# TensorE's order in the attention rounds: the projection piece ahead of the next scores

## The chip, the cores and the metric

One core of a Trainium2 chip runs the whole program. The metric is device time in microseconds (us); lower is better. TensorE (PE) multiplies, VectorE (DVE) and ScalarE (ACT) read its results from PSUM, GpSimd (POOL) works between buffers in SBUF, and SyncE (SP) issues loads. Each engine works off its own instructions in the order in which they stand; semaphores are all that ties the engines to each other.

## The reference, cut to what matters

Two transformer-like blocks run one after the other on 1024 tokens of width 1024, in float32. The change is inside the second block's attention: sixteen heads of width 64, eight of them stick-breaking ("s") and eight forgetting attention ("f").

```
h = rmsnorm_2(x, attn_norm_g)
proj = h @ w_in
# "s" heads, strictly causal:
z = q @ k.T * 0.125
log_one_minus = where(mask, log_sigmoid(-z), 0)
after = cumsum(log_one_minus, reverse=True) - log_one_minus
o = where(mask, exp(log_sigmoid(z) + after), 0) @ v
# "f" heads, causal, F = cumsum(log_sigmoid(f_logit + bias)):
o = softmax(q @ k.T * 0.125 + F[t] - F[s]) @ v
```

## The kernel before, in words

Attention is done in eight **rounds** of two heads each; "s" and "f" rounds take turns, an "s" round first. A round has sixteen **tiles**, eight for each of its two heads: tile t of a head is 128 query rows against (t mod 8) + 1 blocks of 128 keys, so the work grows along eight tiles and falls back at the ninth. While TensorE works on the tiles of one round it also makes the projections (q, k, v) of the next: 18 **pieces** a round, P0 to P17 below, of nine or six matmuls of 512 columns (line 2062). Three pieces make one **half** (512 tokens of q, k or v), and all halves share one PSUM bank, the lower half of G0 (J in the code). VectorE takes a finished half out of it ("evac", line 2478, the rows named `projected<-G`), and the first piece of the next half (P0, P3, P6, P9, P12, P15) waits for that.

The order on TensorE is a loop written out by hand, one turn for each **step** n = 0 to 15 of a round. Before the change a step is: the scores of tile n, two tiles ahead of the one whose weights are due (`scores(s + 2)`; lines 2089, 2090 and the mask 2092); the piece of the step (`PIECE_AT`); the values of tile n - 3 (line 2120); the transposes of tile n - 2 (line 2102). Step 1 has the transposes of v between, step 4 those of the finished round's output (line 2141), and steps 6 and 14 have a second piece, P7 and P16, at their end. Scores alternate between the banks S2 and G1; their first matmul waits until the tile two earlier was read out of the same bank, and at step 5 also until ScalarE has copied the output's transposes (`outT`, line 2307), which use the upper half of G1.

For an "s" tile ScalarE makes 1 - sigmoid (`not_taken`, line 2281; the name reads `forget_sums<-G` for every second tile, which is written to that buffer), VectorE scans it (line 2515), ScalarE makes sigmoid (`taken`, line 2286) when the probability buffer is free, and VectorE multiplies (line 2518). For an "f" tile VectorE adds the forget sums (line 2508, `first`) once GpSimd has put the mask into them (lines 1988, 1990), and ScalarE takes the exponential (line 2292). Either result is what the transposes wait for; ScalarE copies the transposes (`p copied`, line 2275), and the values wait for that.

VectorE's own order has the evacuations between the tiles: the first before the work of tile 2 (step 3), then at steps 6, 8, 11, and 13 in rounds of odd number (14 in even ones), and step 0 of the next. The one of step 8 stands behind the low part of q (line 2486), the one of step 13 or 14 behind the low part of k (line 2493). Rounds here are numbered by the projections under way: in odd rounds (1, 3, 5, 7) the tiles are "s" tiles, in even rounds (2, 4, 6) "f" tiles. Round 0 has pieces only and the last round tiles only.

Of the kernel before, what the change touches and what calls it, by code (L numbers as in the profile page):

```python
# [159 lines left out]
def program(nc, a, out, known):  # L160
# [290 lines left out]
    with nc.Block() as block:  # L451
# [925 lines left out]
        def _(v):  # L1377
# [46 lines left out]
            def exponents(h, w):  # L1424
                s = LEVELS[w - 1]
                me(f"stage {w - 1} k", h)
                fv, fl, fr = block_view(F, s)
                bv, bl, br = block_view(B, s)
                fb, bb = broadcast(fv[:, :, s - 1:s], s), broadcast(bv[:, :, s:s + 1], s)
                _, kl, kr = block_view(E[0], s)  # L1430
                _, ql, qr = block_view(E[1], s)
                v.tensor_tensor(kl, fb, fl, ALU.subtract)
                S.mark("dve", f"exponents {w} 0", v.tensor_tensor(kr, br, bb, ALU.subtract), h)  # L1433
                me(f"stage {w - 1}", h)
                v.tensor_tensor(ql, bb, bl, ALU.subtract)
                S.mark("dve", f"exponents {w} 1", v.tensor_tensor(qr, fr, fb, ALU.subtract), h)
# [192 lines left out]
        @block.gpsimd  # L1629
        def _(g):  # L1630
            split_pair(J_BRB, 0)
            for name, j0, _, _ in BRANCHES:
                splits_of(j0, first=1 if name == "brb" else 0)
# [90 lines left out]
        TILES, STEPS, SHIFT = 2 * TT, 2 * TT * 2 * HEADS, 2  # L1724
# [41 lines left out]
        def tile_of(g):  # L1766

            return X[g // TILES % 2], g % TILES // TT, g % TT
# [11 lines left out]
        def mask_in_sums(g):  # L1780

            return tile_of(g)[0] == "f" and g // TILES < ROUNDS - 1
# [7 lines left out]
        def stream(s):  # L1790

            q, n = divmod(s + SHIFT, TILES)
            return q + 1, n
# [223 lines left out]
        def _(pe):  # L2017
# [25 lines left out]
            def rstd_spread(name, dst, src):  # L2043
                S.wait(pe, "dve", f"{name} diagonals")
                S.mark("pe", f"{name} spread", over_features(halves_of(dst), src))

            def piece(q, p):

                h, part = divmod(p, 3)
                j, half = J_ATT + 3 * q + h // 2, h % 2  # L2050
                bank = FIRST_BANKS[h] if q == 0 else J
                if part == 0:
                    if half == 0:
                        pe.wait_ge(w_ready, j + 1)
                    if q == 0 and h == 2:
                        S.wait(pe, "dve", "f projected")
                    elif q or h > 3:
                        S.wait(pe, "dve", "evac", 6 * q + h - (2 if q == 0 else 1))
                cols = slice(half * NB, half * NB + NB)
                for k in (range(0, 3), range(3, 6), range(6, 8))[part]:  # L2060
                    for w, m, first, last in ((w_hi, A[0], k == 0, False), (w_hi, A[1], False, False), (w_lo, A[0], False, k == KT - 1)):
                        mm = pe.matmul(bank, w[:, j % 2, k, :], m[:, k, cols], start=first, stop=last)  # L2062
                if part == 2 and half == 0:
                    S.mark("pe", "half", mm, 6 * q + h)
                elif part == 2:
                    mm.then_inc(gemm_done, 1)

            def read(g):

                S.wait(pe, *(("dve", "first", g) if tile_of(g)[0] == "f" else ("act", "taken", g)))  # L2070

            def scores(g):

                x, hh, tt = tile_of(g)
                r = g // TILES
                (Qh, Ql, Ks, _), z, w = SETS[r % 2], Z[g % 2], (tt + 1) * P
                if g < 2:
                    S.wait(pe, "act", ("rstd12 copied", "rstd1 copied")[g], 1)
                else:
                    read(g - 2)  # L2080
                if g > TILES and g % TILES == 5:
                    S.wait(pe, "act", "outT", 2 * (r - 1))
                if g % TILES == 0:
                    S.wait(pe, "act", "k high", r)
                    S.wait(pe, "dve", "k low", r)
                t = slice(tt * P, (tt + 1) * P)
                for b in range((w + NB - 1) // NB):
                    cols = slice(b * NB, min(w, (b + 1) * NB))
                    pe.matmul(z[:, cols], Qh[hh][:, t], Ks[hh][:, cols], start=True, stop=False)  # L2089
                    mm = pe.matmul(z[:, cols], Ql[hh][:, t], Ks[hh][:, cols], start=False, stop=mask_in_sums(g) or tt // 4 != b)  # L2090
                if not mask_in_sums(g):
                    mm = pe.matmul(z[:, tt * P:w], identb, maskb[:, "fs".index(x), :], start=False, stop=True)
                S.mark("pe", "z", mm, g)

            def turned(g):

                S.wait(pe, "act" if tile_of(g)[0] == "f" else "dve", "made", g)
                for c, b0, n in GROUP_AT[g]:
                    S.wait(pe, *U_FREE[U_AT["p", c] - 2])
                    bank = bank_of_u(("p", c))  # L2100
                    for b in range(n):
                        mm = pe.transpose(bank[:, b * P:(b + 1) * P], pr[g % 2][:, (b0 + b) * P:(b0 + b + 1) * P], ident)  # L2102
                    S.mark("pe", "turned", mm, c)

            def values(g):


                _, hh, tt = tile_of(g)
                r, at = g // TILES, g % 4 * HD
                v = SETS[r % 2][3]  # L2110
                if g == 0:
                    S.wait(pe, "dve", "evac", 5)
                elif g % 4 == 0:
                    S.wait(pe, "dve", "out", g // 4 - 1)
                if g % TILES == 0:
                    S.wait(pe, "act", "v copied", 2 * r + 1)
                for c, b0, n in GROUP_AT[g]:
                    S.wait(pe, "act", "p copied", c)
                    for b in range(n):
                        mm = pe.matmul(V[:, at:at + HD], pT[c % 2][:, b, :], v[:, b0 + b, own_rows(hh)], start=b0 + b == 0, stop=b0 + b == tt)  # L2120
                    S.mark("pe", "values", mm, c)

            def v_turned(r):
                for half in range(2):
                    S.wait(pe, "dve", "evac", 6 * r + 4 + half)
                    u = U_AT["v", 2 * r + half]
                    if u >= 2:
                        S.wait(pe, *U_FREE[u - 2])
                    for b in range(4):
                        mm = pe.transpose(U[u % 2][:, b * P:(b + 1) * P], qt[:, (4 * half + b) * P:(4 * half + b + 1) * P], ident)  # L2130
                    S.mark("pe", "v turned", mm, 2 * r + half)

            def out_turned(r):
                S.wait(pe, "dve", "out", 4 * r + 3)
                for half in range(2):
                    if ("o", 2 * r + half) in U_AT:
                        S.wait(pe, *U_FREE[U_AT["o", 2 * r + half] - 2])
                    else:
                        read(TILES * (r + 1) - 1)
                    for b in range(4):  # L2140
                        mm = pe.transpose(bank_of_out(r, half)[:, b * P:(b + 1) * P], ON[:, 4 * half + b, :], ident)
                    S.mark("pe", "out turned", mm, 2 * r + half)

            for s in range(-TILES - SHIFT, STEPS):
                q, n = stream(s)
                if 0 <= s + 2 < STEPS:
                    scores(s + 2)
                if q == 0 and n == 0:
                    rstd_spread("rstd12", S2, bs[:, 0, :])
                if q == 0 and n == 3:  # L2150
                    rstd_spread("rstd1", G[1], bs[:, 1, :])
                if q < ROUNDS:
                    piece(q, PIECE_AT[n][0])
                if n == 1 and 1 <= q <= ROUNDS:
                    v_turned(q - 1)
                if s >= 1:
                    values(s - 1)
                if s > TILES and s % TILES == 2:
                    out_turned(s // TILES - 1)
                if s >= 0:  # L2160
                    turned(s)
                if q < ROUNDS:
                    for p in PIECE_AT[n][1:]:
                        piece(q, p)
# [1235 lines left out]
```

## Time and profile before

| | |
|---|---|
| median of 3 runs | 2547.94 us (2546.5 to 2552.3) |
| profiled execution, its own time | 2548.83 us |
| span of its trace | 2547.0 us |
| TensorE matmul busy | 2499.9 us, 98% of the span |
| VectorE, ScalarE, GpSimd busy | 60%, 40%, 42% |
| share of TensorE in the chain that ended last | 83% |
| that chain at the pieces, line 2062 | 10% |
| at the values, line 2120 | 5% |
| granted TensorE clock, mean | 0.996 |

The attention rounds with both pieces and tiles run from about 1233 to 1712 us of the span. A round takes some 68 to 70 us. TensorE's busy time counts a matmul from its start to a modelled end, so matmuls that follow each other overlap in it; how long work holds the engine is better read from one start to the next.

### The profile page before, as it was taken

To read this page: it belongs to the slowest core of one execution; us is meant where nothing else is said; L and a number is where in the kernel's file an instruction comes from. 1 tells how busy PE (TensorE), PEld (TensorE's weight loads), DVE (VectorE), ACT (ScalarE), POOL (GpSimd) and SP (SyncE) were. 2 spreads that over 40 slices of the span, in tenths; PEclk is the share of its full clock that TensorE was granted. 3 is DMA by queue.
4 is the path that set the end of the run, shared out by engine and by line. 5 is a ranking of instruction groups with operands and counts; after the bars stand their busy time and mean duration, and the time that the engine had idled before them with its cause. 6 is when DMAs were issued, how large, how long until landed. Compare 5 with 4: busy or idle time off the path is not lost.

```text
span 2547.0 us, 31625 instructions
## 1 busy us (share of the span) xinstructions
PE 2499.9 (98%) x12610; PEld 2084.2 (82%) x12610; DVE 1519.2 (60%) x1483; ACT 1009.7 (40%) x1416; POOL 1059.3 (42%) x617
## 2 busy tenths in 40 slices
PE   8999999999999999999999999999989999999999
PEld 4888788888788888888888888888868888887887
DVE  4864556665677653444655647375877676675324
ACT  3421044435343431123555556565344444442214
POOL 3665453333433335543121221204557778752320
PEclk9999999999999999999999999999999999999999
DMA  8222231211212134233111101013312222235311
GB/s 338 91 89 73 82 102 50 72 67 67 71 61 76 50 149 174 96 129 106 42 42 34 42 32 44 26 59 133 108 42 100 75 98 77 75 133 215 128 38 67
DMA packets 66238, 226.07 MB, mean 89 GB/s; under 512 B 7816, under 2 KB 11784, under 8 KB 64816
## 3 DMA queue, kind: packets, MB, share of 16 engines
q1 hardware_dynamic: 49824, 169.00, 18.8%
q10 hardware_dynamic: 16272, 55.09, 6.0%
q8 instruction: 99, 1.62, 0.3%
q14 instruction: 43, 0.35, 0.0%
HBM read 174.22 MB, written 45.65 MB: 86 GB/s over the span
## 4 chain that ended last, share of the span: by engine, by line
PE 83%; DVE 8%; issue 3%; ACT 3%; DMA 1%; POOL 1%; SPq 0%; ACTq 0%; DVEq 0%; POOLq 0%
PE G L238 31%; PE G L2897 14%; PE G L2062 10%; PE G L2956 5%; PE G L2120 5%; PE U L2102 2%; PE S L1099 1%; PE S L2968 1%; PE U L2968 1%; PE U L238 1%; PE S L238 1%; PE U L1099 1%; PE G L2089 1%; PE G L2968 1%; PE G L2090 1%
## 5 line engine op out<-in xcount | busy, mean ns | idle before, releaser
L264 POOL TENSOR_TENSOR w_hi<-w_raw,ones 128x1024 fp32r<-128x1024 f32 x67 | 177.7, 2652 | 529.1 <-PE G L238 472.2
L269 POOL TENSOR_TENSOR w_lo<-w_raw,w_hi 128x1024 fp32r<-128x1024 f32 x88 | 238.7, 2712 | 169.4 <-ACT w_hi L263 164.3
L238 PE MATMUL G<-H_hi,w_hi 128*128 128x512 f32 x928 | 290.2, 394 | 1.0 <-ACT silu_zB L724 0.7
L238 PE MATMUL G<-H_lo,w_hi 128*128 128x512 f32 x928 | 285.9, 389 | 0.0
L238 PE MATMUL G<-H_hi,w_lo 128*128 128x512 f32 x928 | 285.8, 389 | 0.0
L238 PEld LDWEIGHTS G<-H_lo,w_hi 128*128 128x128 f32 x928 | 174.2, 188 | 36.5
L238 PEld LDWEIGHTS G<-H_hi,w_lo 128*128 128x128 f32 x928 | 174.2, 188 | 36.4
L238 PEld LDWEIGHTS G<-H_hi,w_hi 128*128 128x128 f32 x928 | 171.6, 188 | 37.0 <-issue 3.7
L1999 POOL TENSOR_TENSOR w_lo<-w_raw,w_hi 128x1024 fp32r<-128x1024 f32 x24 | 59.4, 2473 | 308.9 <-ACT w_hi L2246 308.9
L2120 PEld LDWEIGHTS G<-att_v,probsT 128*128 128x128 f32 x1152 | 146.3, 191 | 12.8 <-ACT probsT L2275 4.0
L2062 PE MATMUL G<-A_hi,w_hi 128*128 128x512 f32 x368 | 152.0, 413 | 3.7 <-DVE projected L2478 3.4
L2120 PE MATMUL G<-att_v,probsT 128*128 128x64 f32 x1152 | 143.9, 270 | 2.5 <-ACT probsT L2275 2.2
L2062 PE MATMUL G<-A_hi,w_lo 128*128 128x512 f32 x368 | 144.4, 392 | 0.0
L2062 PE MATMUL G<-A_lo,w_hi 128*128 128x512 f32 x368 | 143.9, 391 | 0.0
L2275 ACT ACTIVATE probsT<-U 128x512 f32<-128x512 f32 (+1 forms) x192 | 87.1, 488 | 130.5 <-PE U L2102 127.9
L2897 PE MATMUL G<-sums_hi,up_hi_S 128*128 128x512 f32 x260 | 101.5, 390 | 1.0 <-DVE sums_lo L1881 0.5
L2897 PE MATMUL G<-sums_lo,up_hi_S 128*128 128x512 f32 x260 | 101.2, 389 | 0.0
L2897 PE MATMUL G<-sums_hi,up_lo_S 128*128 128x512 f32 x260 | 101.2, 389 | 0.0
L2829 POOL TENSOR_TENSOR up_lo<-up_raw,up_hi 128x512 fp32r<-128x512 f32 x66 | 88.9, 1346 | 13.4 <-ACT up_hi L1916 13.4
L1274 ACT ACTIVATE exps<-exps 128x1024 f32<-128x1024 f32 x60 | 61.9, 1057 | 71.3 <-DVE exps L1433 64.3
L2102 PE MATMUL U<-ident,probs 128*128 128x128 f32 x576 | 84.8, 274 | 0.0
L2062 PEld LDWEIGHTS G<-A_hi,w_hi 128*128 128x128 f32 x368 | 69.8, 190 | 16.0 <-issue 2.5
(605 smaller groups left out, 6247.3 us busy)
## 6 DMA issues: line engine op xcount, KB each, us to landing
w_raw<-w_in SPq DMA_DIRECT2D x65, 512.0 KB, 3.3
up_raw<-w_up SPq DMA_DIRECT2D x44, 512.0 KB, 4.9
pre_raw<-w_in SPq DMA_DIRECT2D x30, 512.0 KB, 3.3
act_d<-made SPq DMA_DIRECT2D x22, 512.0 KB, 2.9
wm<-w_mod SPq DMA_DIRECT2D x8, 1024.0 KB, 18.4
w_raw<-w_out SPq DMA_DIRECT2D x16, 512.0 KB, 3.4
x_d<-x ACTq DMA_DIRECT2D x16, 512.0 KB, 2.9
x<-x_d SPq DMA_DIRECT2D x16, 512.0 KB, 9.1
```

What stands on the lines that cost most here:

```text
L238: mm = nc.tensor.matmul(dst[:, n * NB:n * NB + c], w[:, k, :], m[:, k, n * NB:n * NB + c], start=first, stop=last)
L264: eng.tensor_tensor(dst, src, ones.unsqueeze(1).to_broadcast([P, kt, P]), ALU.mult)
L269: nc.gpsimd.tensor_tensor(w_lo[:, slot, 0:kt, :], w_raw[:, slot, 0:kt, :], w_hi[:, slot, 0:kt, :].bitcast(F32), ALU.subtract).then_inc(w_r ...
L1274: S.mark("act", f"exps {w} {e}", act.activation(E[e], src, ACT.Exp, scale=1.0 / GATE_NORM), h)
L2062: mm = pe.matmul(bank, w[:, j % 2, k, :], m[:, k, cols], start=first, stop=last)
L2102: mm = pe.transpose(bank[:, b * P:(b + 1) * P], pr[g % 2][:, (b0 + b) * P:(b0 + b + 1) * P], ident)
L2120: mm = pe.matmul(V[:, at:at + HD], pT[c % 2][:, b, :], v[:, b0 + b, own_rows(hh)], start=b0 + b == 0, stop=b0 + b == tt)
L2275: S.mark("act", "p copied", act.activation(pT[c % 2][:, 0:n, :], blocks_of(bank_of_u(("p", c)), n), ACT.Copy), c)
L2829: S.mark("pool", f"low {name}", g_.tensor_tensor(slot_lo[name], slab_source(p, name), slot_hi[name].bitcast(F32), ALU.subtract), p)
L2897: mm = pe.matmul(dst, w[name][:, j, :], up_moving(name, x, j), start=first and j == 0 and w is slot_hi and x == 0, stop=j == PAIRS_OF - 1 ...
L2956: mm = pe.matmul(dst[:, halves[n]], w[:, slot, k, :], m[:, k, halves[n]], start=k == 0 and w is w_hi and m is parts[0], stop=k == KT - 1 a ...
L2968: mm = pe.matmul(PAIRS[t % 3][:, halves[n]], H[x][:, f, t * P:(t + 1) * P], w[f][:, halves[n]], start=f == 0 and x == 0 and w is row_hi, s ...
```

## The change

In each step the piece of the next round's projections is issued ahead of the scores of the second next tile, not behind them. The rest stays: the instructions, their waits and the order on all other engines. Only rounds 1 to 7 have both a piece and scores in a step, 112 steps in all.

```
             for s in range(-TILES - SHIFT, STEPS):
                 q, n = stream(s)
-                if 0 <= s + 2 < STEPS:
-                    scores(s + 2)
                 if q == 0 and n == 0:
                     rstd_spread("rstd12", S2, bs[:, 0, :])
                 if q == 0 and n == 3:
                     rstd_spread("rstd1", G[1], bs[:, 1, :])
                 if q < ROUNDS:
                     piece(q, PIECE_AT[n][0])
+                if 0 <= s + 2 < STEPS:
+                    scores(s + 2)
                 if n == 1 and 1 <= q <= ROUNDS:
                     v_turned(q - 1)
```

TensorE, step 6 of round 3 (an "s" round), before: the four transposes of tile 3 that end step 5 (line 2102), the scores of tile 6 into S2, and the start of P6. The waits stand behind a row.

```order
L2102 MATMUL U<-ident,probs_8707 128x128 [waits act_steps,dve_steps]
L2102 MATMUL U<-ident,probs_8707 128x128 x3
L2089 MATMUL S<-k_parts_8703,q_hi_8699 128x512 [waits act_steps]
L2090 MATMUL S<-k_parts_8703,q_lo_8701 128x512
L2089 MATMUL S<-k_parts_8703,q_hi_8699 128x384
L2090 MATMUL S<-k_parts_8703,q_lo_8701 128x384
L2092 MATMUL S<-bf_constants 128x128
L2062 MATMUL G<-A_hi,w_hi 128x512 [waits dve_steps,w_ready]
```

The same place in the changed kernel, up to the first matmul of the scores:

```order
L2102 MATMUL U<-ident,probs_8707 128x128 [waits act_steps,dve_steps]
L2102 MATMUL U<-ident,probs_8707 128x128 x3
L2062 MATMUL G<-A_hi,w_hi 128x512 [waits dve_steps,w_ready]
L2062 MATMUL G<-A_lo,w_hi 128x512
L2062 MATMUL G<-A_hi,w_lo 128x512
L2062 MATMUL G<-A_hi,w_hi 128x512
L2062 MATMUL G<-A_lo,w_hi 128x512
L2062 MATMUL G<-A_hi,w_lo 128x512
L2062 MATMUL G<-A_hi,w_hi 128x512
L2062 MATMUL G<-A_lo,w_hi 128x512
L2062 MATMUL G<-A_hi,w_lo 128x512
L2089 MATMUL S<-k_parts_8703,q_hi_8699 128x512 [waits act_steps]
```

The wait for VectorE, the evacuation of the half before, now comes directly behind the transposes, with no scores between.

TensorE, step 14 of round 4 (an "f" round), before: the end of the transposes of step 13, the scores of tile 14, which wait for VectorE, and the start of P15, which does too.

```order
L2102 MATMUL U<-ident,probs_8707 128x128 x3
L2089 MATMUL S<-k_parts_8687,q_hi_8683 128x512 [waits dve_steps]
L2090 MATMUL S<-k_parts_8687,q_lo_8685 128x512
L2089 MATMUL S<-k_parts_8687,q_hi_8683 128x384
L2090 MATMUL S<-k_parts_8687,q_lo_8685 128x384
L2062 MATMUL G<-A_hi,w_hi 128x512 [waits dve_steps]
```

And in the changed kernel:

```order
L2102 MATMUL U<-ident,probs_8707 128x128 x3
L2062 MATMUL G<-A_hi,w_hi 128x512 [waits dve_steps]
L2062 MATMUL G<-A_lo,w_hi 128x512
L2062 MATMUL G<-A_hi,w_lo 128x512
L2062 MATMUL G<-A_hi,w_hi 128x512
L2062 MATMUL G<-A_lo,w_hi 128x512
L2062 MATMUL G<-A_hi,w_lo 128x512
L2062 MATMUL G<-A_hi,w_hi 128x512
L2062 MATMUL G<-A_lo,w_hi 128x512
L2062 MATMUL G<-A_hi,w_lo 128x512
L2089 MATMUL S<-k_parts_8687,q_hi_8683 128x512 [waits dve_steps]
```

Both waits are still there, in the other order. The orders of VectorE, ScalarE, GpSimd and SyncE are the same in both kernels.

## Rows read from the trace of the kernel before

**Rows 1.** The page: busy time of TensorE, and its granted clock in 40 slices.

```profile
PE 2499.9 (98%) x12610; PEld 2084.2 (82%) x12610; DVE 1519.2 (60%) x1483; ACT 1009.7 (40%) x1416; POOL 1059.3 (42%) x617
...
PEclk9999999999999999999999999999999999999999
```

**Rows 2.** Waits of TensorE, 1230 to 1710 us: total, times, longest (us).

```profile
PE G L2062 <- DVE projected L2478: 3.4, 7, 0.7
PE S L2089 <- DVE row_mins L2508: 1.5, 3, 0.5
```

**Rows 3.** Timeline, TensorE, round 3, steps 5 and 6: start, duration, instruction, idle before.

```profile
1386.74 0.49 PE L2102 MATMUL U<-ident,probs 128*128 128x128 f32 x3
1387.39 0.47 PE L2089 MATMUL G<-k_parts,q_hi 128*128 128x512 f32 x1 [0.17 <-ACT att_outT L2307]
...
1390.64 0.48 PE L2089 MATMUL S<-k_parts,q_hi 128*128 128x512 f32 x1
...
1391.55 0.23 PE L2092 MATMUL S<-bf_constants 128*128 128x128 bf16 x1
1392.24 0.47 PE L2062 MATMUL G<-A_hi,w_hi 128*128 128x512 f32 x1 [0.47 <-DVE projected L2478]
```

**Rows 4.** Timeline, ScalarE, the same place.

```profile
1388.34 0.70 ACT L2281 ACTIVATE not_taken<-S 128x640 f32<-128x640 f32 x1 [0.51 <-ACT att_outT L2307]
1388.94 0.48 ACT L2275 ACTIVATE probsT<-U 128x384 f32<-128x384 f32 x1
```

**Rows 5.** Timeline, VectorE, the same place.

```profile
1389.08 1.49 DVE L2515 TENSOR_TENSOR_SCAN left_over<-not_taken 128x640 f32<-128x640 f32 x1 [4.07 <-ACT not_taken L2281]
1390.67 0.82 DVE L2518 TENSOR_TENSOR probs<-probs,left_over 128x640 f32<-128x640 f32 x1
1391.42 0.68 DVE L2478 SCALAR_TENSOR_TENSOR projected<-G,rstd 128x512 f32<-128x512 f32 x1
```

**Rows 6.** Timeline, TensorE, round 3, step 8.

```profile
1401.93 0.30 PE L2089 MATMUL S<-k_parts,q_hi 128*128 128x128 f32 x1
...
1402.24 0.48 PE L2062 MATMUL G<-A_hi,w_hi 128*128 128x512 f32 x1
```

**Rows 7.** Timeline, VectorE, the same place.

```profile
1401.44 0.69 DVE L2478 SCALAR_TENSOR_TENSOR projected<-G,rstd 128x512 f32<-128x512 f32 x1
```

**Rows 8.** Timeline, TensorE, round 3, step 14.

```profile
1424.83 0.48 PE L2089 MATMUL S<-k_parts,q_hi 128*128 128x512 f32 x1
...
1425.94 0.50 PE L2062 MATMUL G<-A_hi,w_hi 128*128 128x512 f32 x1
```

**Rows 9.** Timeline, VectorE, the same place.

```profile
1420.56 4.55 DVE L2493 TENSOR_TENSOR k_parts<-projected,k_parts 64x1024 fp32r<-64x1024 f32 x2
1425.20 0.69 DVE L2478 SCALAR_TENSOR_TENSOR projected<-G,rstd 128x512 f32<-128x512 f32 x1
```

**Rows 10.** Timeline, GpSimd, the same place.

```profile
1420.41 2.39 POOL L1999 TENSOR_TENSOR w_lo<-w_raw,w_hi 128x1024 fp32r<-128x1024 f32 x1 [16.80 <-ACT w_hi L2246]
```

**Rows 11.** Timeline, VectorE, round 4, steps 7 and 8: the second part of q's low part.

```profile
1469.05 1.22 DVE L2486 TENSOR_TENSOR q_lo<-projected,q_hi 64x1024 fp32r<-64x1024 f32 x1 [2.23 <-ACT q_hi L2255]
```

**Rows 12.** Timeline, TensorE, round 4, steps 3 and 8.

```profile
1449.11 0.48 PE L2089 MATMUL G<-k_parts,q_hi 128*128 128x512 f32 x1
...
1471.11 0.50 PE L2062 MATMUL G<-A_hi,w_hi 128*128 128x512 f32 x1 [0.42 <-DVE projected L2478]
```

**Rows 13.** Timeline, VectorE, round 4, step 3.

```profile
1448.53 0.69 DVE L2478 SCALAR_TENSOR_TENSOR projected<-G,rstd 128x512 f32<-128x512 f32 x1
```

**Rows 14.** Timeline, TensorE, round 4, end of step 13 and step 14.

```profile
1492.69 0.61 PE L2102 MATMUL U<-ident,probs 128*128 128x128 f32 x4
1493.83 0.50 PE L2089 MATMUL S<-k_parts,q_hi 128*128 128x512 f32 x1 [0.53 <-DVE row_mins L2508]
...
1494.76 0.40 PE L2062 MATMUL G<-A_hi,w_hi 128*128 128x512 f32 x1
```

**Rows 15.** Timeline, VectorE, the same place.

```profile
1493.69 0.69 DVE L2478 SCALAR_TENSOR_TENSOR projected<-G,rstd 128x512 f32<-128x512 f32 x1
```

**Rows 16.** Timeline, TensorE, start of round 1: P0.

```profile
1234.75 0.47 PE L2062 MATMUL G<-A_hi,w_hi 128*128 128x512 f32 x1 [0.73 <-DVE projected L2478]
```

**Rows 17.** Timeline, TensorE, round 3: P7 behind transposes, scores behind P7, values behind P6.

```profile
1394.40 1.00 PE L2120 MATMUL G<-att_v,probsT 128*128 128x64 f32 x8
...
1395.71 0.48 PE L2062 MATMUL G<-A_hi,w_hi 128*128 128x512 f32 x1
...
1397.88 0.39 PE L2089 MATMUL G<-k_parts,q_hi 128*128 128x512 f32 x1
```

**Rows 18.** Timeline, TensorE, last round, which has no pieces: values behind scores.

```profile
1730.67 1.07 PE L2120 MATMUL G<-att_v,probsT 128*128 128x64 f32 x8
```

More of the change, by code:

```diff
@@ L2145, in _ @@
                 q, n = stream(s)
-                if 0 <= s + 2 < STEPS:
-                    scores(s + 2)
                 if q == 0 and n == 0:
@@ L2153, in _ @@
                     piece(q, PIECE_AT[n][0])
+                if 0 <= s + 2 < STEPS:
+                    scores(s + 2)
                 if n == 1 and 1 <= q <= ROUNDS:
```

## The prediction

> **What bounds the kernel now.** I read the page first: TensorE is busy 98% of the span and its clock is at the higher level, 2.4 GHz, in every slice [rows 1]. So the time is TensorE's work plus its stops, and a change of order can only move the stops. The second view is TensorE's waits in the rounds that change: 3.4 us in seven waits of a piece for an evacuation, 1.5 us in three waits of scores for VectorE [rows 2]. Those numbers are too small, since a matmul's modelled end covers part of a stop; I take stops from start to start. The third view is the timelines of TensorE, VectorE and ScalarE at the places with a stop, one odd round (3, "s" tiles) and one even round (4, "f" tiles). The pattern repeats: seven piece waits are one at the start of round 1, one in each of rounds 3, 5, 7 at step 6 and one in each of rounds 2, 4, 6 at step 8. The reader is to see in each place which engine's row ends just before TensorE goes on, and what hangs before that row.
>
> **What is moved, and what that does in principle.** 112 steps swap a piece (nine matmuls, about 2.1 us) and scores (0.3 to 0.95 us). Nothing is added or removed, and no other queue changes. Two waits change places. Scores now ask for their bank some 2 us later, so their stops go. The first piece of a half asks for its bank sooner by the scores' time, since that no longer stands between the transposes and it. Where the evacuation is not ready, the scores used to fill the wait; now TensorE stops, and the scores come on top. The half itself is finished earlier by the same scores' time, so an evacuation that waited only for TensorE comes earlier too, and nothing is lost. What decides is therefore whether an evacuation waits for TensorE or for its place in VectorE's queue.
>
> **Odd rounds, step 6.** The evacuation starts at 1391.42 straight behind the multiply and scan of tile 4 [rows 5]; the scan began when `not_taken` of tile 4 was there, and that stood behind the output copy on ScalarE [rows 4]. The half had been ready for more than 1.5 us. So P6 can't start before 1392.24, whatever TensorE does in front of it. Before, the scores (1390.64 to 1391.59, 0.95 us) filled part of the stop and 0.65 us was left [rows 3]. After, P6 starts where it did and the scores follow: +0.95. The stop of 0.35 us at step 5 (transposes end about 1387.04, scores start 1387.39 [rows 3]) goes, but nothing is won: the values of step 5 want the copy that ends at 1389.42 [rows 4], and P6 waits for the same evacuation.
>
> **Odd rounds, step 8.** The evacuation ends at 1402.13 and P9 starts at 1402.24 [rows 6, 7]: it is just in time with 0.31 us of scores in front. Its queue place hangs on the high part of q, on the copies behind the transposes of step 6, all shifted with TensorE. So P9 keeps its distance and the scores come behind: +0.31.
>
> **Odd rounds, step 14.** The low part of k holds VectorE for 4.55 us to 1425.11, the evacuation ends at 1425.89 and P15 starts at 1425.94 [rows 8, 9]. The scores from 1424.83 were nearly the whole cover (0.95 us and a stop of 0.16). After, P15 starts there all the same: +0.95. Three places make 2.2 us for each of rounds 3, 5, 7: 6.6 us.
>
> **Round 1.** It has no output copy, and its step 6 is just in time either way (0 to 0.1). P0 waits 0.73 us for the evacuation of round 0 [rows 16], with 0.3 us of scores in front that now come behind; steps 8 and 14 are as above: 0.3 + 0.31 + 0.95, about 1.5 us.
>
> **Even rounds.** Step 3: the evacuation ends at 1449.22 [rows 13], and the transposes end at 1449.11 [rows 12]: P3 stops for about 0.2. Step 5: the stop for the output copy, 0.35 as in rows 3, goes, and here VectorE and ScalarE are idle enough that it stays won: -0.35. Step 8: P9 is fixed by the evacuation behind q's low part, which ends at 1470.27 [rows 11, 12]: the scores, 0.25 without a mask, come on top. Step 14: the scores stopped until 1493.83, while the transposes ended about 1493.05, a stop of 0.8 [rows 14]. That stop goes, but the evacuation ends at 1494.38 [rows 15]; P15 starts at 1494.49 in place of 1494.76 and the scores (0.93) follow: +0.66. Sum 0.2 - 0.35 + 0.25 + 0.66 = 0.76, times three, 2.3 us.
>
> **The changeover itself.** The first matmul behind short transposes lasts 0.48 against 0.39 behind a piece, be it a piece or scores [rows 3, 17]; a piece behind masked scores pays the same, and now the values behind scores do, 1.07 against 1.00 for eight [rows 17, 18]. Two such costs a step before, two after: I take 0, with bounds of 0.03 us a step either way, 3 us over 112 steps.
>
> **What else is late.** Scores finish 2.1 us later, so `not_taken` does. Its next reader, the scan, mostly waits for VectorE's queue, and the multiply waits for `taken`, which needs the transposes two steps back, as before. About a whole step of 4 us lies between a multiply's end and its transposes, so I price this at 0.
>
> **Sum.** 6.6 + 1.5 + 2.3 = 10.4 us. The profiled execution took 2548.83 us for a span of 2547.0, 0.9 above the median of 2547.94; added to the median, 2558.4 us, +0.41%.
>
> **A rule against a row.** At step 14 of odd rounds the two parts of k's low part last 4.55 us while GpSimd's 2.39 us subtraction begins just before them [rows 9, 10]; a like part alone takes 1.22 us [rows 11]. The Trainium skill ("SBUF — State Buffer", section "Who interferes with whom") says that a VectorE instruction with two SBUF inputs and a GpSimd instruction that reads SBUF exclude each other. By that rule, the trace agrees: 4.55 is about 2 x 1.22 and the rest of the 2.39. Both instructions hang on the same copies of step 11, so I expect the meeting to stay. If it did not, see the second rival.
>
> **The rivals.**
> - *Evacuations come earlier* and the removed stops are a gain. Price: stops of 0.35 and 0.65 in three odd rounds, 0.35, 0.6 and 0.8 in three even ones, and 0.9 at the start are 9.2 us: 2538.7. For it: the halves are ready earlier. Against it: in rows 5, 9 and 15 VectorE takes the half only when its own queue is through. Chance 0.05.
> - *GpSimd and VectorE no longer meet*, or the chain at step 6 shortens by as much: the evacuation at step 14 would end some 2 us earlier, four terms of 0.95 fall away, 3.8 us; with the lower changeover bound as well it is about 2552. Chance 0.13, two thirds of it no measurable change.
> - *The change of order does nothing*: if evacuations moved with the scores everywhere, gains and losses cancel within 2 us: 2548 to 2550. For it: no work is added. Chance 0.06.
> - *Late scores reach the transposes.* In odd rounds VectorE is the second busiest; if the 2.1 us by which `not_taken` comes later were passed on to the multiply of a large tile, TensorE would stop at its transposes. It decides once more than the 4 us of slack are used up; one stop of 2 to 3 us in each odd round is 8 to 12 us more, 2568. Chance 0.06.
>
> **How the numbers follow.** The forecast, 2554 to 2563, has 0.70. Range 2551 to 2566: it takes in the changeover bounds and most of the second rival, and leaves out some 0.15. A measurement of this kernel tells about 0.2%, 5.1 us, from no change, so "same" ends at 2553.0: faster 0.05, same 0.14, slower 0.81.
>
> **What would show it.** In the profile after: no waits of scores for VectorE or for the output copy; waits of pieces for `projected` grown from 3.4 to about 13 us, at step 6 of rounds 3, 5, 7 about 1.6 us each, at step 14 of rounds 1 to 7 about 1.1 to 1.4 each, at step 8 0.3 to 0.9; evacuations at the same distance from the work that led to them. A whole round 3 longer by 2.2, round 4 by 0.8. The forecast is wrong if the evacuation at step 6 or 14 moves ahead, or if transposes begin to wait.

## The result, and the profile after

| | before | after |
|---|---|---|
| median | 2547.86 us (10 runs, 2546.5 to 2552.3) | 2560.05 us (10 runs, 2558.35 to 2572.9) |
| span of the profiled execution | 2547.0 us | 2556.6 us |
| TensorE busy | 2499.9 us | 2500.5 us |
| granted clock, mean | 0.996 | 0.996 |

The changed kernel takes 1.0049 of the time before, interval 1.0039 to 1.0059: 12.5 us more, between 10 and 15 (the two medians differ by 12.2). The forecast was 2558.4, in a range of 2551 to 2566.

TensorE's waits between 1230 and 1710 us, the answer to [rows 2], as engine and line, what it waited for, total, times and longest (us). Beside the two rows of [rows 2] the kernel before has one for the output copy,

```profile
PE G L2089 <- ACT att_outT L2307: 0.8, 5, 0.2
```

and one of 0.3 us. The changed kernel has a single row:

```profile
PE G L2062 <- DVE projected L2478: 14.4, 15, 1.4
```

No scores wait any more in these rounds, neither for VectorE nor for the output copy, and the pieces' waits for the evacuation have grown from 3.4 to 14.4 us.

Step 6 of round 3 in the timeline of TensorE (start, duration, instruction, idle before), beside [rows 3]:

```profile
1388.59 0.61 PE L2102 MATMUL U<-ident,probs 128*128 128x128 f32 x4
1390.64 0.47 PE L2062 MATMUL G<-A_hi,w_hi 128*128 128x512 f32 x1 [1.44 <-DVE projected L2478]
...
1391.60 0.63 PE L2062 MATMUL G<-A_hi,w_hi 128*128 128x512 f32 x1
...
1394.16 0.58 PE L2089 MATMUL S<-k_parts,q_hi 128*128 128x512 f32 x1
1394.58 0.39 PE L2090 MATMUL S<-k_parts,q_lo 128*128 128x512 f32 x1
```

and the same place on VectorE, beside [rows 5]:

```profile
1387.47 1.49 DVE L2515 TENSOR_TENSOR_SCAN left_over<-not_taken 128x640 f32<-128x640 f32 x1 [3.46 <-ACT not_taken L2281]
1389.06 0.82 DVE L2518 TENSOR_TENSOR probs<-probs,left_over 128x640 f32<-128x640 f32 x1
1389.81 0.68 DVE L2478 SCALAR_TENSOR_TENSOR projected<-G,rstd 128x512 f32<-128x512 f32 x1
```

VectorE's scan, multiply and evacuation follow each other as before. The transposes end about 1388.95 (an estimate, since their ends are modelled) and P6 starts at 1390.64: a stop of 1.7 us with nothing in it, then the piece, then the scores. Counted from the start of the round, P6 starts where it did, 19.7 us into it in both kernels. The other two kinds of place, steps 14 and 8, in rounds 3 and 4, beside [rows 8, 12, 14]:

```profile
1427.06 0.50 PE L2062 MATMUL G<-A_hi,w_hi 128*128 128x512 f32 x1 [0.90 <-DVE projected L2478]
...
1472.87 0.50 PE L2062 MATMUL G<-A_hi,w_hi 128*128 128x512 f32 x1 [0.59 <-DVE projected L2478]
...
1496.44 0.50 PE L2062 MATMUL G<-A_hi,w_hi 128*128 128x512 f32 x1 [1.14 <-DVE projected L2478]
```

The best measure of a place is the length of a round, since other stages of the program differ by a few us from one execution to the next (the attention rounds began 3.3 us earlier in this trace, in a part of the program that the change leaves alone: before them the clock was at its lower level for some 10 us in the trace of before, about 50 and 1190 us, and for some 3 in this one). A round is taken here from its transposes of v (step 1) to the next one's. For round 3 these are, in the kernel before,

```profile
1372.56 0.71 PE L2130 MATMUL U<-ident,projected 128*128 128x128 f32 x5
...
1442.34 0.93 PE L2130 MATMUL U<-ident,projected 128*128 128x128 f32 x7
```

and in the changed kernel

```profile
1370.93 0.83 PE L2130 MATMUL U<-ident,projected 128*128 128x128 f32 x6
...
1444.40 0.82 PE L2130 MATMUL U<-ident,projected 128*128 128x128 f32 x6
```

that is 69.78 and 73.47 us. All kernels of this study, those of the experiments below (e1 to e12) included, read in the same way (us; odd rounds have "s" tiles, even rounds "f" tiles; the last column is the sum less that of before):

| kernel | 1 | 2 | 3 | 4 | 5 | 6 | 7 | sum |
|---|---|---|---|---|---|---|---|---|
| before | 64.44 | 68.78 | 69.78 | 68.82 | 69.80 | 68.87 | 67.04 | |
| changed | 65.64 | 69.20 | 73.47 | 69.26 | 71.90 | 69.44 | 69.14 | +10.5 |
| e1, first pieces | 66.05 | 69.69 | 71.92 | 69.81 | 71.94 | 69.95 | 69.20 | +11.0 |
| e2, other pieces | 64.41 | 68.33 | 69.71 | 68.38 | 69.74 | 68.34 | 66.93 | -1.7 |
| e3, step 6 | 64.48 | 68.86 | 70.68 | 68.94 | 70.72 | 68.92 | 67.95 | +3.0 |
| e4, step 14 | 65.36 | 69.33 | 70.73 | 69.42 | 70.71 | 69.42 | 67.96 | +5.4 |
| e12, step 8 | 64.70 | 69.00 | 70.07 | 69.06 | 70.04 | 69.05 | 67.33 | +1.7 |
| e5 | 65.71 | 69.23 | 70.35 | 69.23 | 70.37 | 69.41 | 67.61 | +4.4 |
| e6 | 64.52 | 67.75 | 70.78 | 67.84 | 70.74 | 67.91 | 69.62 | +1.6 |
| e7 | 69.87 | 67.97 | 73.41 | 68.03 | 72.02 | 68.12 | 72.49 | +14.4 |
| e8 | 64.23 | 67.55 | 68.83 | 67.55 | 68.80 | 67.55 | 66.07 | -7.0 |
| e9 | 65.12 | 68.06 | 69.95 | 68.13 | 69.97 | 68.13 | 67.18 | -1.0 |
| e10 | 64.19 | 67.55 | 68.85 | 67.54 | 68.83 | 67.54 | 66.06 | -7.0 |
| e11 | 64.54 | 67.77 | 69.23 | 67.83 | 69.24 | 67.95 | 66.47 | -4.5 |

Where the clock stays up, rounds 3 and 5 of a kernel agree within 0.05 us and rounds 2, 4 and 6 within 0.3. Round 3 of the changed kernel stands out: it is 1.6 us longer than round 5. TensorE's granted clock there, by stretches of 4 us (stretch, its length, busy time of PE, PEld, DVE, ACT and POOL with their instructions, granted clock, DMA share, GB/s):

```profile
1386.00:1390.00 4.00, 3.07 (x20) 2.42 (x18) 2.43 (x3) 3.37 (x7) 0.00 (x0) 1.00 0.32 131
1390.00:1394.00 4.00, 3.36 (x9) 2.73 (x10) 3.11 (x3) 2.65 (x3) 0.00 (x0) 0.64 0.35 131
1394.00:1398.00 4.00, 4.00 (x25) 3.40 (x25) 1.67 (x2) 2.15 (x4) 0.00 (x0) 0.93 0.00 0
...
1532.00:1536.00 4.00, 2.63 (x12) 2.22 (x13) 3.84 (x4) 3.38 (x4) 0.00 (x0) 1.00 0.36 119
```

Shortly after the stop of 1.7 us the clock was at its lower level, 1.2 GHz: matmuls of 512 columns start 0.43 us apart there, not 0.23, and P6 took 3.52 us (1390.64 to 1394.16) where P15 of the same kernel takes 2.18. That is 1.3 us, nearly all of the excess. At the same stop in round 5 (last row) it stayed at 1.00.

**The last round differs as well.** It has no pieces, so the change doesn't reach it, but from its transposes of v to its last values it takes 44.9 us in the trace of before and 48.1 in that of the changed kernel. VectorE's instruction of line 2541 has two inputs in SBUF, and it meets GpSimd's subtraction of line 2005. Before, VectorE starts first and GpSimd is the longer one:

```profile
1744.25 1.43 DVE L2541 SCALAR_TENSOR_TENSOR x<-x,par,rstd 128x1024 f32<-128x1024 f32 x1
```

```profile
1744.67 3.24 POOL L2005 TENSOR_TENSOR A_lo<-A_lo,A_hi 128x1024 fp32r<-128x1024 f32 x1
```

In the changed kernel GpSimd starts first, VectorE takes twice as long, and TensorE's scores stop for it:

```profile
1751.09 2.37 POOL L2005 TENSOR_TENSOR A_lo<-A_lo,A_hi 128x1024 fp32r<-128x1024 f32 x1
```

```profile
1751.52 3.02 DVE L2541 SCALAR_TENSOR_TENSOR x<-x,par,rstd 128x1024 f32<-128x1024 f32 x1
```

```profile
1755.20 0.51 PE L2089 MATMUL G<-k_parts,q_hi 128*128 128x512 f32 x1 [1.54 <-DVE row_mins L2508]
```

Behind that stop the clock fell as well (0.57 from 1756 to 1760 us). Which engine starts first hangs on a load of 0.5 MB for which GpSimd waits; it took 6.5 us from issue to landing in the trace of before and 5.6 in the other. It is not tied to the order on TensorE: of the fourteen traces of this study only those of before, e2 and e12 have VectorE first, and e7 and e9, which have the order of before, don't.

### The profile page after: what moved, and what is told of

The parts are those of the page before. It is cut to its first block and busy times, and to the rows that moved or that the text cites. A ratio compares the mean times of both kernels' runs of the same rounds, so it can differ in the third digit from the quotient of the medians.

```text
span 2556.6 us, 31625 instructions
## 1 busy us (share of the span) xinstructions
PE 2500.5 (98%) x12610; PEld 2085.9 (82%) x12610; DVE 1521.1 (59%) x1483; ACT 1012.4 (40%) x1416; POOL 1058.7 (41%) x617
## 5 line engine op out<-in xcount | busy, mean ns | idle before, releaser
L2062 PE MATMUL G<-A_hi,w_hi 128*128 128x512 f32 x368 | 154.9, 421 | 15.1 <-DVE projected L2478 14.4
```

## The experiments

In kernels with added lines the same instruction has a line number up to five higher than in the rows of before.

**Which steps cost (e1 to e4, e12).** Theory: the loss sits at the first pieces of halves, where the evacuation is late. Rival: scores that finish 2 us later delay the tile's work, in all steps. Each kernel is the one before with this edit, and another condition in each:

```
+                ahead = n in (0, 3, 6, 8, 11, 14)
-                if 0 <= s + 2 < STEPS:
+                if not ahead and 0 <= s + 2 < STEPS:
                     scores(s + 2)
...
                     piece(q, PIECE_AT[n][0])
+                if ahead and 0 <= s + 2 < STEPS:
+                    scores(s + 2)
```

e1, the swap at the six steps that begin a half:

> The piece goes ahead of the scores only at steps 0, 3, 6, 8, 11 and 14, where the piece is the first of a half and waits for an evacuation; elsewhere the scores go first as before. Theory (the scores no longer cover the wait for the evacuation): nearly the whole loss, +10 to +13 us on the kernel before, a bit more than the changed kernel since the output copy's stop at step 5 of even rounds stays. TensorE's waits for `projected` about 14 us. Rival (scores that finish later delay the tile's work on ScalarE and VectorE, a loss spread over all steps): about 6 of 16 steps' share, +4 to +5 us.

Measured: 2559.63 us against 2549.48 before, 1.0039 (1.0028 to 1.0050); rounds +11.0 us, waits of the pieces:

```profile
PE G L2062 <- DVE projected L2481: 13.6, 14, 1.4
```

e2, the swap at the other ten steps:

> The other half of the change: the piece goes ahead at the ten steps of a round whose piece waits for nothing. Theory: no loss; the stop for the output copy at step 5 of even rounds goes, -1.1 us; 2546 to 2549. TensorE's waits for `projected` stay at 3.4 us in seven. Rival (late scores): +7 to +8 us, 2555.

Measured: 2545.93 us, 0.9989 (0.9979 to 0.9998); rounds -1.7 us, even ones -0.44 to -0.53 each. The pieces' waits are nearly those of before (3.7 us for 3.4); the output copy's are gone, VectorE's for scores are not (step 14 is not among these steps):

```profile
PE G L2062 <- DVE projected L2481: 3.7, 7, 0.7
PE S L2089 <- DVE row_mins L2511: 1.6, 3, 0.5
PE G L2089 <- ACT probs L2289: 0.3, 1, 0.3
```

So the rival falls: 70 of the 112 swapped steps cost nothing, and even give a little back.

e3, the swap at step 6 alone:

> The piece goes ahead at step 6 alone. Theory: rounds 3, 5, 7 lose the width of the scores, 0.95 us each, +2.9 us, and now and then 1.4 us more where TensorE's clock falls to its lower level after the stop of about 1.7 us: 2551 to 2553. Even rounds and round 1 unchanged. If the clock falls for another reason than this stop, the granted clock is 1.00 through steps 6 of all rounds.

Measured: 2553.18 us, 1.0009 (0.9999 to 1.0019); rounds 3, 5 and 7 +0.90, +0.92, +0.91, the rest within 0.12. The granted clock was 1.00 through step 6 of all three rounds, though the stops of 1.7 us were there, so this run neither shows nor rules out that such a stop brings the clock down. e4, at step 14 alone:

> The piece goes ahead at step 14 alone. Theory: +0.95 us in rounds 1, 3, 5, 7 and +0.66 in rounds 2, 4, 6, +5.8 us together: 2553 to 2555, with a stop of 0.9 to 1.2 us before P15 in every round. Rival (late scores): 1 of 16 steps' share, +0.7 us.

Measured: 2554.25 us, 1.0016 (1.0006 to 1.0026); odd rounds +0.91 to +0.95, even ones +0.55 to +0.60. e12, at step 8 alone:

> The piece goes ahead at step 8 alone, nothing else changed. Theory: +0.31 us in rounds 1, 3, 5, 7 and +0.25 in rounds 2, 4, 6, 2.0 us together; a measurement hardly tells it from no change, but the lengths of the rounds in the trace do.

Measured: 2551.97 us, 1.0015 (1.0005 to 1.0025), where the rounds grew by 1.7 us, within the interval of 1.3 to 6.4; the trace measures it better, and it has +0.24 to +0.29 in odd rounds and +0.18 to +0.24 in even ones. The parts add up: 3.0 + 5.4 + 1.7 - 1.7 is 8.4, and what e1 has beyond e3, e4 and e12 (steps 0, 3 and 11, not run alone) is 0.9. The sum, which is e1 and e2 together, is 9.3 us, while the changed kernel has 10.5 with 1.3 to 1.4 of lower clock.

**What the evacuations wait for (e5, e6).** Theory: for their place in VectorE's queue, and at step 14 for GpSimd. Both are the changed kernel with one edit. e5:

```
-        EVAC_AT = [{3: 0, 6: 1, 8: 2, 11: 3, at: 4} for at in (14, 13)]
+        EVAC_AT = [{3: 0, 5 if at == 13 else 6: 1, 8: 2, 11: 3, at: 4} for at in (14, 13)]
```

> The changed kernel, with VectorE's second evacuation of odd rounds ahead of the work of tile 4 (its step 5) in place of behind it (step 6). It tests that P6 stops for the place in VectorE's queue and not for the half. Theory: the stop before P6 in rounds 3, 5, 7 goes (about 1.6 us each) and with it the chance of a lower clock right behind it; other stops stay: 4.8 us less than the changed kernel, about 2554; the waits for `projected` fall from 14.4 to about 10 us. Rival (late scores): no gain, and P6 still stops, now for `not_taken` and the scan.

Measured: 2553.30 us, 1.0012 (0.9998 to 1.0027) of before, some 7 us less than the changed kernel by the medians; the stops before P6 are gone (longest wait now 1.1 us, that of step 14), rounds 5 and 7 are 1.5 us shorter than in the changed kernel and round 3, where the clock didn't fall, 3.1:

```profile
PE G L2062 <- DVE projected L2478: 10.5, 14, 1.1
```

e6:

```
-                j = J_ATT + 3 * q + {1: 1, 7: 2, 12: 3}.get(n, KT * KT)
+                j = J_ATT + 3 * q + {1: 1, 7: 2, 13: 3}.get(n, KT * KT)
                 if J_ATT + 2 <= j <= J_OUT2 + 1:
+                    if n == 13:
+                        S.wait(g, "dve", "k low", q)
```

> The changed kernel, with GpSimd's third weight split of a round behind VectorE's low part of k (and behind the masking of tile 12), not beside it. It tests that P15 stops because k's low part and, in even rounds, the masking are held up by that split. Theory: k's two parts take 2.4 us in place of 4.55, the evacuation of step 14 ends early, and the stops before P15 (0.9 us in odd rounds, 1.1 to 1.3 in even ones) go: 7 to 8 us less than the changed kernel, about 2552. Rival (only queue order counts, not the meeting of the engines): k's parts stay at 4.5 us and nothing is gained in odd rounds.

Measured: 2551.02 us, 1.0007 (0.9997 to 1.0018), 9 us less than the changed kernel. On VectorE the two parts of k's low part take 2.46 us, and the evacuation now waits only for TensorE; GpSimd's split starts behind them and meets a scan in their place, which takes 2.92 us here:

```profile
1417.43 2.46 DVE L2495 TENSOR_TENSOR k_parts<-projected,k_parts 64x1024 fp32r<-64x1024 f32 x2
1420.16 0.69 DVE L2480 SCALAR_TENSOR_TENSOR projected<-G,rstd 128x512 f32<-128x512 f32 x1 [0.28 <-PE G L2064]
1420.77 2.92 DVE L2517 TENSOR_TENSOR_SCAN left_over<-not_taken 128x640 f32<-128x640 f32 x1
```

```profile
1419.96 2.38 POOL L2001 TENSOR_TENSOR w_lo<-w_raw,w_hi 128x1024 fp32r<-128x1024 f32 x1 [19.77 <-DVE k_parts L2495]
```

In the changed kernel the same scan, which meets no split, takes 1.48:

```profile
1426.92 1.48 DVE L2515 TENSOR_TENSOR_SCAN left_over<-not_taken 128x640 f32<-128x640 f32 x1
```

In even rounds the cause is another one. There k's two parts take 2.45 us in the changed kernel already, and the split starts only as they end. What is late is the masking of a tile (lines 1988 and 1990), which stands behind the split in GpSimd's own queue; VectorE waits for it, and its evacuation with it:

```profile
1491.83 2.47 POOL L1999 TENSOR_TENSOR w_lo<-w_raw,w_hi 128x1024 fp32r<-128x1024 f32 x1 [4.29 <-ACT w_hi L2246]
```

```profile
1494.95 0.82 DVE L2508 CUSTOM_DVE_ANT_0 probs<-not_taken,S 128x640 f32<-128x640 f32 x1 [2.91 <-POOL not_taken L1990]
```

In e6 the masking goes ahead of the split, and the evacuation of round 4 starts 49.3 us into the round and not 51.3.

Rounds 1 and 5 are 1.1 us shorter than in the changed kernel, the even ones 1.4 to 1.5, and round 3, where the clock didn't fall, 2.7. Round 7 is 0.5 longer, for here the clock fell in its turn, behind the stop before P6, which e6 leaves in place; P6 takes 3.60 us (1665.19 to 1668.79):

```profile
1665.19 0.47 PE L2064 MATMUL G<-A_hi,w_hi 128*128 128x512 f32 x1 [1.45 <-DVE projected L2480]
...
1668.79 0.52 PE L2091 MATMUL S<-k_parts,q_hi 128*128 128x512 f32 x1
```

```profile
1664.00:1668.00 4.00, 2.81 (x8) 2.22 (x9) 3.67 (x4) 3.20 (x4) 0.00 (x0) 0.70 0.38 128
```

The Trainium skill ("SBUF — State Buffer", section "Who interferes with whom") states that a VectorE instruction with two SBUF inputs contends with a GpSimd instruction that reads SBUF, and that the port pair they share is an exclusive lock. By that rule a meeting can be moved to another instruction, but not halved. The trace agrees: the scan that now meets the split takes 2.92 us against 1.48, and k's low part, which no longer does, 2.46 against 4.54.

**The order of before with both edits (e7), and the split order with both (e8).**

> The order of the kernel before with the edits of e5 and e6 together. Theory: its remaining stops at step 6 (0.65, odd) and step 14 (0.16 odd, 0.8 even) go: 5 us less than before.

Measured: 2563.28 us, 1.0050 (1.0037 to 1.0064), 20 us above what was expected. The place is step 8 of odd rounds. TensorE, VectorE and GpSimd there:

```profile
1406.62 0.80 PE L2064 MATMUL G<-A_hi,w_hi 128*128 128x512 f32 x1 [2.89 <-DVE projected L2480]
```

```profile
1400.26 1.09 DVE L2520 TENSOR_TENSOR probs<-probs,left_over 128x896 f32<-128x896 f32 x1
1401.27 4.51 DVE L2488 TENSOR_TENSOR q_lo<-projected,q_hi 64x1024 fp32r<-64x1024 f32 x2
1405.87 0.69 DVE L2480 SCALAR_TENSOR_TENSOR projected<-G,rstd 128x512 f32<-128x512 f32 x1
```

```profile
1402.12 2.58 POOL L2001 TENSOR_TENSOR w_lo<-w_raw,w_hi 128x1024 fp32r<-128x1024 f32 x1 [22.36 <-ACT w_hi L2248]
```

Before, the same two instructions overlapped too, but VectorE was first: the second half of q's low part started at 1400.13, 0.65 us ahead of the split, and it was GpSimd that took longer, 2.83 us:

```profile
1400.78 2.83 POOL L1999 TENSOR_TENSOR w_lo<-w_raw,w_hi 128x1024 fp32r<-128x1024 f32 x1 [23.02 <-ACT w_hi L2246]
```

In e7 the early evacuation comes ahead of tile 4's scan. Counted from the start of the round, q's low part starts 0.36 us later and the split 0.66 us sooner, so that the split is now first by 0.38 us: 4.51 us for what took 2.44 (the expectation of e9 below says that q's low part had become earlier against the split; it had become later). During or just behind the stops of 2.9 us the clock fell in rounds 1, 3 and 7; here rounds 3, 5 and 7:

```profile
1406.00:1410.00 4.00, 3.38 (x9) 2.70 (x10) 3.90 (x3) 0.00 (x0) 0.00 (x0) 0.57 0.31 119
...
1544.00:1548.00 4.00, 1.16 (x12) 1.02 (x10) 3.91 (x3) 2.33 (x5) 2.13 (x1) 1.00 0.18 54
...
1688.00:1692.00 4.00, 3.81 (x14) 3.20 (x15) 3.79 (x4) 0.00 (x0) 0.00 (x0) 0.70 0.26 94
```

> The order of e2 (piece ahead only where it waits for nothing) with the edits of e5 and e6 together. Theory: the gains of e2 (1.6 us in its rounds) and of e7 (5 us) add up, about 6 to 7 us less than the kernel before, the fastest of all.

Measured: 2542.94 us, 0.9978 (0.9967 to 0.9989); rounds -7.0 us, as expected. With the scores behind P5 the half is ready some 1 us sooner, and so is the early evacuation (16.1 us into round 3, 17.4 in e7). The second half of q's low part starts 0.54 us ahead of the split again, so the split waits (2.93 us) and VectorE doesn't.

**Taking the second meeting away as well (e9 to e11).** The edit, on e7, e8 and e5 with e6:

```
-                j = J_ATT + 3 * q + {1: 1, 7: 2, 13: 3}.get(n, KT * KT)
+                j = J_ATT + 3 * q + {1: 1, 8: 2, 13: 3}.get(n, KT * KT)
...
-                    if n == 13:
-                        S.wait(g, "dve", "k low", q)
+                    if n in (8, 13):
+                        S.wait(g, "dve", "q low" if n == 8 else "k low", q)
```

> The kernel of e7 (order of before, early evacuation, third split late) with GpSimd's second weight split of a round behind VectorE's low part of q as well. e7 was slower since q's low part, now some 1 us earlier on VectorE relative to that split, ran into it (4.51 us for two parts in place of 2.44) and P9 stopped 2.9 us. Theory (the meeting of the two engines alone made e7 slow): the parts take 2.4 us again, the stop goes, 2541 to 2544. Rival (something else in the early evacuation costs): it stays above 2555.

Measured: 2546.82 us, 0.9991 (0.9982 to 1.0001): 16 us below e7, so the meeting and what followed from it made e7 slow, but 2.8 us above the upper end of what I expected (2541 to 2544). q's low part is back at 2.44 us; P9 still stops, for 0.83 us at most in the modelled ends:

```profile
PE G L2064 <- DVE projected L2480: 5.3, 8, 0.8
```

The early evacuation waits for P5, which stands behind the scores in this order; tile 4's scan waits with it, and VectorE runs without a pause from there to the evacuation of step 8 (12 us in round 3). On the order of before the early evacuation thus gives odd rounds nothing: round 3 is 69.95 us against 69.78.

> The same third edit on the kernel of e8. Theory: e8 had no such meeting worth a stop, so within 2 us of e8, 2541 to 2543.

Measured: 2541.73 us, 0.9966 (0.9955 to 0.9978), the lowest median of the study, 6.1 us below the kernel before by the medians and 5.6 to 11.5 by the interval; its rounds are those of e8 within 0.1 us, and the intervals of the two overlap: they are not told apart.

> The order of the changed kernel with the three edits. Theory (the swap costs only where an evacuation is late): with the evacuations of steps 6 and 14 early the swap costs nothing there; what stays is step 8 (0.3 in odd, 0.25 in even rounds) and the start of round 1 (0.2): 2 to 3 us above e9 and e10, 2543 to 2546. Rival (late scores cost in every step): 8 us or more above e9.

Measured: 2543.16 us, 0.9981 (0.9972 to 0.9991); rounds 2.5 us above e10, as expected, but 3.5 below e9, which I had put beside e10. What is left are waits at step 8 and at the start:

```profile
PE G L2064 <- DVE projected L2480: 3.6, 8, 1.0
```

So the very order that costs 9 us in this kernel is better than the order before (by 3.5 us in the rounds, e11 against e9) once the evacuations are in time.

## Why the prediction was right, point by point

- **Odd rounds, 2.2 us each.** Measured 2.10 in rounds 5 and 7. Step 6: 0.95 predicted, 0.91 by e3. Step 8: 0.31 and 0.24 to 0.29 (e12). Step 14: 0.95 and 0.91 to 0.95 (e4). In each the added time is about the width of the scores, since TensorE's restart is fixed by VectorE. The evacuations stood still: counted from the start of round 3 that of step 6 begins at 18.86 us before and at 18.86 in e3, that of step 8 at 28.88 and 28.87 in e12, that of step 14 at 52.64 and 52.63 in e4. For steps 6 and 14, e5 and e6 show it from the other side, since they free VectorE and leave TensorE's order alone; for step 8 no run does.
- **Round 1, 1.5 us**, of which 0.3 lies before the first transposes of v. Measured 1.20 in the rest, 1.26 predicted; the early part grew by 0.2 (from P0 to those transposes 4.59 us before, [rows 16], and 4.78 after).
- **Even rounds, 0.76 us each.** Measured 0.42 to 0.57, the term that was sized worst. Step 14 was 0.66, measured 0.55 to 0.60; the gain outside the first pieces was 0.35, measured 0.44 to 0.53 (e2). Step 8 was 0.25, measured 0.18 to 0.24 (e12); step 3 was 0.2, and what e1 has beyond e3, e4 and e12 in even rounds is 0.03 to 0.30. The mechanism stands: e6 takes 1.4 to 1.5 us from each even round by letting step 14's evacuation go early.
- **Changeover, 0 with 3 us either way.** The even terms of e2, a swap at ten steps with one known stop, leave -0.01 us a step. The bound was wide.
- **Late scores, 0.** Shown by e2, and by e11 against e9.
- **The clock and the last round.** The prediction had no term for either, and that is where the forecast is short: the rounds have 9.1 us without round 3's fall, 10.5 with it, while the medians differ by 12.2. The prediction read the clock as being at its higher level in every slice, but a slice is 64 us and its digit says 90% or more: a fall of a few us doesn't show in it, and the mean of 0.996 already told that there were some. That the total came within 2 us of the forecast is in part luck: the rounds gave about 1 us less than forecast, and what was left out gave more.
- **The signs.** Waits of pieces 14.4 us for 13 forecast, no waits of scores, 1.44 us at step 6 for 1.6 and 0.59 at step 8 of even rounds for 0.3 to 0.9. At step 14 it was 1.14 us in even rounds, within the 1.1 to 1.4 that were named, but 0.90 in odd ones, below them. Round 4 grew by 0.44 us and not 0.8, round 3 by 3.69 with the fall of the clock; round 5, without one, by 2.10 for 2.2.
- **The second rival**, that GpSimd and VectorE would not meet, did not come true: k's two parts took 4.54 us in round 3 of the changed kernel as well. e6 shows what it would have been worth: 8.9 us in the rounds (10.5 less 1.6, each with one fall of the clock), 1.1 in each odd round and 1.4 to 1.5 in each even one, which the rival had left out. In the even rounds, though, it is GpSimd's own queue and not the meeting.

What stays open is the rest of the time. In the two traces the rounds account for 10.5 us and the last round for 3.2, and the other stages, which differ from execution to execution, for some 4 us the other way. The 9.1 us and the last round's 3.2 would come near the 12.2 of the medians, but a trace is one execution; how often the load lands early enough in either kernel wasn't recorded, and so it stays open whether the change has a part in it. The execution of 2572.9 us of the changed kernel has a mean clock of 0.990, and one of 2560.32 us of the kernel before 0.991.

That a stop brings the clock down was not shown by a run made for it, but the last round bears on it. In the three traces in which VectorE is first there the scores don't stop and the clock doesn't fall (44.8 to 45.1 us for the round). In the eleven others the scores stop for 1.2 to 1.7 us, and the clock falls at that place in eight: not in e1, e10 and e11 (46.2 to 46.7 us), for some 3 us in the changed kernel and in e5 to e9 (47.7 to 48.2), and for 27 in e3 and e4 (56.6 and 56.8). In e3 it fell at about 1749 us:

```profile
1748.11 0.51 PE L2089 MATMUL G<-k_parts,q_hi 128*128 128x512 f32 x1 [1.18 <-DVE row_mins L2511]
```

```profile
1748.00:1752.00 4.00, 3.71 (x17) 3.34 (x18) 2.23 (x6) 2.24 (x6) 0.00 (x0) 0.65 0.00 0
...
1772.00:1776.00 4.00, 4.00 (x14) 3.04 (x14) 0.60 (x2) 0.80 (x4) 0.00 (x0) 0.50 0.00 0
```

## What to carry to other kernels

Before moving work on the busiest engine ahead of other work, ask of each wait that it passes whether it is for this engine's own result or for a place in another engine's queue. Work that stands in front of a wait of the second kind is free as long as the wait is longer than the work. Moved behind the wait, it costs its full width, less what its own wait had cost before (0.9 us at step 14 of odd rounds, but 0.55 to 0.60 in even ones, where the scores had stopped too). The cure is on the other engine: take the half out early, keep GpSimd's and VectorE's two-input instructions apart at the places where TensorE waits behind VectorE, and keep what VectorE waits for ahead of long work in GpSimd's queue; then the order that lost here wins.

## What the runs showed of the hardware that was not expected

- TensorE's clock went to 1.2 GHz behind some stops of 1.7 us (round 3 of the changed kernel and round 7 of e6; not at the ten other stops before P6 in rounds 3, 5 and 7 of the changed kernel, e1, e3 and e6), at three of four stops of 2.9 us in e7, and behind eight of eleven stops of 1.2 to 1.7 us in the last round. A fall in the rounds cost 1.3 us on top of a stop of 1.7; in e3 and e4 one in the last round lasted 27 us and made that round 10 us longer than the same stop without a fall.
- When GpSimd's subtraction (2.4 us) starts first and a VectorE instruction with two inputs in SBUF comes upon it, VectorE's takes 1.4 to 2.1 us longer (1.48 to 2.92, 2.44 to 4.51, 2.46 to 4.54). When VectorE's starts first, GpSimd's does (2.39 to 2.83 at q's low part, 2.37 to 3.24 in the last round). A scan is hit as well as a subtraction, and a shift of 1 us between the two queues, or a load that lands 0.9 us sooner, is enough to change which of them waits.
